# Two joined layers: plain transposes behind row scaling, pairs of attention items, and feed-forward norms applied as r squared behind the second product

## The reference, cut to what matters

```python
# first layer
proj = rmsnorm(x, g_mix_pre) @ w_in            # fq, fk, fv, f_logit, cq, ck, cv
# fox: logits[t,s] = q_t.k_s * scale + c[t] - c[s] (causal), 8 heads of 64
# chk: logits = q.k * scale + rel_bias(table), 8 heads of 64
y = concat([rmsnorm(y_fox, g_fox_out), rmsnorm(y_chk, g_chk_out)])
x = x + rmsnorm(y @ w_out, g_mix_post)
x = x + rmsnorm(attention(rmsnorm(x) @ w_mq, mem_n @ w_mk, mem_n @ w_mv) @ w_mo, g_mem_post)
h = rmsnorm(x, g_ff_pre)
y = jnp.square(jax.nn.relu(h @ w_ff1)) @ w_ff2
x = x + rmsnorm(y, g_ff_post)
# second layer: gated delta rule with a short convolution, sparse attention (dsa) with
# selected keys, two gates, then
x = x + merged @ w_out
h2 = rms_norm(x, norm_mlp_g)
x = x + jnp.square(jax.nn.relu(h2 @ w_mlp_up)) @ w_mlp_down
```

## Time and profile before

| | |
|---|---|
| median of 3 runs | 1035.77 us (1030.82 to 1036.05) |
| the profiled execution, its own time | 1035.79 us |
| its span in the profile | 1034.0 us |
| PE busy | 976.3 us (94%) |
| DVE busy | 589.5 us (57%) |
| ACT busy | 513.9 us (50%) |
| POOL busy | 178.7 us (17%) |
| mean granted clock of PE in the span | 0.98 |

### The profile page before, as it was taken

The page is one execution under the profiler, slowest core; times in us unless marked ns, Lnnn a source line. Parts: engine busy times, 40 slices in busy tenths (PEclk is TensorE's granted clock), DMA queues, the critical chain, the costliest instruction groups (busy, mean ns, idle before and its releaser), DMA issues.

```text
span 1034.0 us, 15468 instructions
## 1 busy us (share of the span) xinstructions
PE 976.3 (94%) x6056; PEld 859.3 (83%) x6056; DVE 589.5 (57%) x921; ACT 513.9 (50%) x910; POOL 178.7 (17%) x171
## 2 busy tenths in 40 slices
PE   5999999999999999999999498999899889999998
PEld 5998876778789998887779497788799879998886
DVE  4353445564466665345578888685554657665342
ACT  4454455564465544335556555754345446544331
POOL 0011000010010000001018888600455200000000
PEclk9998999999999999999999799998999999999999
DMA  9664223244255666563635233263110055655552
GB/s 326 204 196 130 82 82 122 83 157 147 82 162 164 192 196 201 170 199 123 203 113 174 82 123 124 86 200 122 41 42 2 1 163 163 196 172 198 170 201 81
DMA packets 99703, 146.75 MB, mean 142 GB/s; under 512 B 2480, under 2 KB 57904, under 8 KB 99504
## 3 DMA queue, kind: packets, MB, share of 16 engines
q1 hardware_dynamic: 99632, 145.78, 43.6%
HBM read 144.72 MB, written 1.05 MB: 141 GB/s over the span
## 4 chain that ended last, share of the span: by engine, by line
PE 43%; issue 42%; DVE 8%; POOL 2%; ACT 2%; DVEq 1%; DMA 1%; POOLq 1%; SPq 0%; ACTq 0%
PE acc L429 5%; PE acc L430 5%; PE acc L431 5%; PE acc L441 5%; PE acc L442 5%; PE acc L443 5%; DVE s_w_lo L379 3%; PE aux L1509 2%; DVE s_qkvT L1279 1%; ACT s_w_hi L373 1%; PE acc L467 1%; PE acc L468 1%; PE acc L469 1%; PE aux L1439 1%; DMA s_w_raw<-in_w_in 1%
## 5 line engine op out<-in xcount | busy, mean ns | idle before, releaser
L379 DVE TENSOR_TENSOR s_w_lo<-s_w_raw,s_w_hi 128x2048 fp32r<-128x2048 f32 (+1 forms) x195 | 312.5, 1609 | 211.3 <-ACT s_w_hi L373 211.0
L373 ACT ACTIVATE s_w_hi<-s_w_raw 128x2048 fp32r<-128x2048 f32 (+1 forms) x195 | 263.8, 1361 | 144.5 <-PE acc L431 117.5
L441 PE MATMUL acc<-s_h_hi,s_w_hi 128*128 128x256 f32 x800 | 229.4, 287 | 3.1 <-DVE s_h_lo L612 1.8
L442 PE MATMUL acc<-s_h_lo,s_w_hi 128*128 128x256 f32 x800 | 227.4, 284 | 0.0
L443 PE MATMUL acc<-s_h_hi,s_w_lo 128*128 128x256 f32 x800 | 227.3, 284 | 0.0
L441 PEld LDWEIGHTS acc<-s_h_hi,s_w_hi 128*128 128x128 f32 x800 | 154.1, 193 | 4.2 <-DVE s_w_lo L379 2.0
L442 PEld LDWEIGHTS acc<-s_h_lo,s_w_hi 128*128 128x128 f32 x800 | 154.1, 193 | 0.1
L443 PEld LDWEIGHTS acc<-s_h_hi,s_w_lo 128*128 128x128 f32 x800 | 154.1, 193 | 0.0
L430 PE MATMUL acc<-s_w_lo,s_hid_hi 128*128 128x512 f32 x224 | 89.5, 400 | 0.0
L429 PE MATMUL acc<-s_w_hi,s_hid_hi 128*128 128x512 f32 x224 | 88.4, 395 | 0.0
L431 PE MATMUL acc<-s_w_hi,s_hid_lo 128*128 128x512 f32 x224 | 87.8, 392 | 0.0
(11 more groups left out here) (300 smaller groups left out, 1682.7 us busy)
## 6 DMA issues: line engine op xcount, KB each, us to landing
s_w_raw<-in_w_in SPq DMA_DIRECT2D x44, 1024.0 KB, 5.2
s_w_raw<-in_w_ff SPq DMA_DIRECT2D x32, 1024.0 KB, 5.2
s_w_raw<-in_w_mlp_up SPq DMA_DIRECT2D x16, 1024.0 KB, 5.4
s_w_raw<-in_w_mlp_down SPq DMA_DIRECT2D x16, 1024.0 KB, 5.1
s_w_raw<-in_w_out SPq DMA_DIRECT2D x8, 1024.0 KB, 5.1
s_w_raw<-in_w_mk SPq DMA_DIRECT2D x4, 1024.0 KB, 5.0
s_w_raw<-in_w_mv SPq DMA_DIRECT2D x4, 1024.0 KB, 5.1
s_w_raw<-in_w_mq SPq DMA_DIRECT2D x4, 1024.0 KB, 5.2
```

What stands on the lines that cost most here:

```text
L373: act.activation(w_hi[u % SPLIT_SLOTS][:, cs], w_raw[u % RAW_SLOTS][:, cs], ACT.Copy).then_inc(w_hi_done, 4 if q is None else 1)
L379: dve.tensor_tensor(w_lo[u % RAW_SLOTS][:, cs], w_raw[u % RAW_SLOTS][:, cs], w_hi[u % SPLIT_SLOTS][:, cs].bitcast(F32), ALU.subtract).then ...
L441: pe.matmul(o, wh[:, cs], hi[:, k, :], start=k == 0, stop=False)
L442: pe.matmul(o, wh[:, cs], lo[:, k, :], start=False, stop=False)
```

## The change

1. **Norms of x at first and of `mem`.** DVE multiplies the rows by r (128x1024, two instructions) and PE does 16 plain transposes in place of 16 matmuls with the diagonal. At the start ACT and DVE split unit 0 in quarters, with the first rows' split between them, and unit 1 behind.
2. **Fox bias.** The second matmul of each fox item goes. Four matmuls (`fb_pe`, 8 rows, 512 columns) stand between the quarters of cv's second unit, and DVE adds the mask to them once (`fb_dve`), into a bias that the items read.
3. **Attention in pairs.** Items are ordered by tile, then head, and go in pairs: two score products, v products of the pair before the last, transposes of the last pair, then two quarters of weights (three in dsa). Copy and reciprocal are one instruction per pair.
4. **Norm of y by tiles.** Tile 0's squares, scaling and transposes lie in the attention; `out` units 0 and 1 run tile by tile with tile 1's norm between. Memory attention ends likewise before `mo`.
5. **Turns mo to ff1 and out2 to up.** The rows are transposed without r; only the gain is applied (`gain_act`, `gain_dve`). The squares come after the gains, POOL makes r squared (`r2_pool`), and it scales behind `ff2` and `down`. The transposes lie inside the last pair of products.
6. **Delta rule.** Unit 1 of gb moves from behind the back part to between the four `dt_pe` blocks, and a gate (`GATES[9]`) is computed earlier.

```diff
+        def gain_act(act, n, t, g):
+            N.wait(act, nt_tr)
+            for c in range(4):
+                k = 4 * g + c
+                act.activation(h_hi[:, k, t * P:(t + 1) * P], tile_bank(t, g)[:, c * P:(c + 1) * P], ACT.Copy,
+                               scale=gcol[:, GAIN[n], k:k + 1]).then_inc(nt_hi, 1)
...
+        def r2_pool(pool, n, t):
+            c = 4 * NCOL[n] + t
+            pool.wait_ge(ss_done, squares_until(n, 1, t))
+            pool.tensor_scalar(stat[:, c:c + 1], stat[:, c:c + 1], stat[:, c + 2:c + 3], EPS, ALU.add, ALU.add)
+            pool.drain()
+            pool.tensor_tensor(r2_col(n, t), stat[:, c:c + 1], minus1[:], ALU.pow)
+            pool.drain()
+            pool.tensor_scalar(r2_col(n, t, 2), r2_col(n, t), ROOT_D, None, ALU.mult).then_inc(r2_done, 1)
...
+        def nt_dve_scale(dve, n, src, dst):
+            for t in range(NT):
+                N.wait(dve, rstd_done)
+                c = 4 * NCOL[n] + t
+                dve.tensor_scalar(dst[:, t, :], src[:, t, :], rstd[:, c:c + 1], None, ALU.mult).then_inc(diag_done, 1)
...
-                        if GAIN[n] is None:
-                            i = pe.transpose(o, piece, ident())
-                        else:
-                            g = k // 4 if n == "y" else 0
-                            i = pe.matmul(o, piece, diag[:, 2 * g + t, :], start=True, stop=True)
+                        i = pe.transpose(o, piece, ident())
...
+        def y_dve_scale(dve, t, g):
+            N.wait(dve, rstd_done)
+            c = 4 * NCOL["y"] + 2 * t + g
+            piece = y[:, t, g * 512:(g + 1) * 512]
+            dve.tensor_scalar(piece, piece, rstd[:, c:c + 1], None, ALU.mult).then_inc(diag_done, 1)
+        def y_pe(pe, t, g):
+            N.wait(pe, diag_done)
+            for c in range(4):
+                k = 4 * g + c
+                i = pe.transpose(Y_BANK[t][g][:, c * P:(c + 1) * P], y[:, t, k * P:(k + 1) * P], ident())
+            i.then_inc(nt_tr, 1)
...
+            pe.wait_ge(p_done, i + 2)
+            if i:
+                pe.wait_ge(ptc_done, i)
+            nb = it["nk"] // P
+            for j in range(2):
+                for b in range(nb):
+                    m = pe.transpose(PT_BANK[:, (j * nb + b) * P:(j * nb + b + 1) * P], bufs(i)[1][:, (i + j) % 3, b * P:(b + 1) * P], ident())
+            m.then_inc(pt_done, 2)
...
-                                      qk=[(fqT[r:r + 64, m, ts], fkT[r:r + 64, m, 0:nk]), (sel_l[r:r + 40, h, ts], sel_r[r:r + 40, 0:nk])],
-                                      bias=cst[:, C_CAUSAL + 2 * P - nk:C_CAUSAL + 2 * P],
...
+                    items.append(dict(nk=nk, scale=1.0, dv=FD, qk=[(fqT[r:r + 64, m, ts], fkT[r:r + 64, m, 0:nk])],
+                                      bias=foxb[:, h, :] if t else xn[:, 1, h * P:(h + 1) * P],
...
+        def fb_pe(pe, between):
+            for j in range(4):
+                pe.matmul(FB_BANK[j][:], sel_a[0:8, 0:P], sel_l[0:8, 2 * j:2 * j + 2, :], start=True, stop=True).then_inc(fb_mm, 1)
+                between(j)
...
+        def fb_dve(dve):
+            for j in range(4):
+                dve.wait_ge(fb_mm, j + 1)
+                b = FB_BANK[j][:].rearrange("p (h s) -> p h s", h=2)
+                dve.tensor_tensor(xn[:, 1, 2 * j * P:(2 * j + 2) * P].rearrange("p (h s) -> p h s", h=2), b[:, :, 0:P],
+                                  both(cst[:, C_CAUSAL + P:C_CAUSAL + 2 * P]), ALU.add)
+                dve.tensor_tensor(foxb[:, 2 * j:2 * j + 2, :], b, both(cst[:, C_CAUSAL:C_CAUSAL + 2 * P]), ALU.add).then_inc(fb_done, 1)
...
+                dve.scalar_tensor_tensor(xn[:, t, cs], acc[b][:], r2_col("ff", t), gpost[:, cs], ALU.mult, ALU.mult).then_inc(acc_free[b], 1)
...
+        def ff_act(act, tag, post, pre):
+            last = of[tag][-1]
+            for u in of[tag][:-2]:
+                advance_hi(act, u)
+            post_stats(act, post, tag, 0)
+            advance_hi(act, last - 1)
+            post_stats(act, post, tag, 1, [0])
+            for q in (0, 1):
+                advance_hi(act, last, q)
+            for g in range(2):
+                gain_act(act, pre, 0, g)
+            post_stats(act, post, tag, 1, [1])
+            for q in (2, 3):
+                advance_hi(act, last, q)
+            for g in range(2):
+                gain_act(act, pre, 1, g)
+            act.wait_ge(x_done, 2 * NT * 2)
+            for t in range(NT):
+                for g in range(2):
+                    square(act, pre, g, t, x[:, t, g * 512:(g + 1) * 512])
...
-            for i in range(len(items) + 3):
-                if i < len(items):
-                    at_pe_scores(pe, i0 + i, items[i])
-                if 2 <= i <= len(items) + 1:
-                    at_pe_tr(pe, i0 + i - 2, items[i - 2])
-                if i >= 3:
-                    at_pe_pv(pe, i0 + i - 3, items[i - 3])
-                between(i)
+            n = len(items) // 2
+            for p in range(n + 2):
+                if p < n:
+                    for j in (2 * p, 2 * p + 1):
+                        at_pe_scores(pe, i0 + j, items[j])
+                if p >= 2:
+                    at_pe_pv(pe, i0 + 2 * p - 4, items[2 * p - 4:2 * p - 2])
+                if 1 <= p <= n:
+                    at_pe_tr(pe, i0 + 2 * p - 2, items[2 * p - 2])
+                between(p)
...
+        def fox_parts(p):
+            lo, hi = [min(4 * len(MEMU), max(0, 2 * k - 1)) for k in (p, p + 1)]
+            return [(MEMU[q // 4][0], MEMU[q // 4][1], q % 4) for q in range(lo, hi)]
...
-            for u in range(AHEAD):
-                unit_hi(act, u)
+            for q in range(4):
+                unit_hi(act, 0, q)
             act.wait_ge(gain_in, 16)
             nt_act(act, "mix", h_hi)
+            for u in range(1, AHEAD):
+                unit_hi(act, u)
...
+                if p == len(FOX) // 4 + 2:
                     act.wait_ge(y_done, len(FOX) // 2)
-                    for t in range(NT):
-                        square(act, "y", 0, t, y[:, t, 0:512])
+                    for g in range(2):
+                        square(act, "y", g, 0, y[:, 0, g * 512:(g + 1) * 512])
+                if p == 3 * len(FOX) // 8 + 2:
+                    act.wait_ge(y_done, 3 * len(FOX) // 4)
+                    square(act, "y", 0, 1, y[:, 1, 0:512])
+                if p == len(FOX) // 2:
+                    for g in range(2):
+                        y_act(act, 0, g)
...
-                wait_added(act, "out2", 0, t)
-                square(act, "mlp2", 0, t, x[:, t, 0:512])
-            wait_added(act, "out2", 1, 0)
-            square(act, "mlp2", 1, 0, x[:, 0, 512:D])
             for q in (0, 1):
                 advance_hi(act, of["out2"][-1], q)
-            wait_added(act, "out2", 1, 1)
-            square(act, "mlp2", 1, 1, x[:, 1, 512:D])
-            nt_tile_act(act, "mlp2", h_hi, 0, range(KC))
+            for g in range(2):
+                gain_act(act, "mlp2", 0, g)
             for q in (2, 3):
                 advance_hi(act, of["out2"][-1], q)
-            nt_tile_act(act, "mlp2", h_hi, 1, range(KC))
+            for g in range(2):
+                gain_act(act, "mlp2", 1, g)
+            for t in range(NT):
+                for g in range(2):
+                    wait_added(act, "out2", g, t)
+                    square(act, "mlp2", g, t, x[:, t, g * 512:(g + 1) * 512])
...
-            nt_dve_diag(dve, "mix")
-            for u in range(AHEAD):
+            nt_dve_scale(dve, "mix", x, xn)
+            for j in range(2):
+                for q in (2 * j, 2 * j + 1):
+                    unit_lo(dve, 0, q)
+                nt_dve(dve, "mix", h_hi, h_lo, (2 * j, 2 * j + 1))
+            for u in range(1, AHEAD):
...
+            def x_tile(tag, t):
+                for g in range(2):
+                    if tag == "mo":
+                        pe.wait_ge(x_done, 2 * NT + 2 * t + g + 1)
+                    else:
+                        wait_added(pe, tag, g, t)
+                    quad_pe(pe, tile_bank(t, g), x, t, g)
...
+            tile_mm(pe, u0, 0, h_hi, h_lo, fresh)
+            y_pe(pe, 1, 0)
+            tile_mm(pe, u1, 0, h_hi, h_lo, fresh)
             pe.wait_ge(y_done, len(FOX))
-            nt_pe(pe, "y", y, (2, 3))
-            normed[0] += KC
-            mm("out", 0, 1, fresh=True)
+            y_pe(pe, 1, 1)
+            tile_mm(pe, u0, 1, h_hi, h_lo, fresh).then_inc(unit_done, 1)
+            tile_mm(pe, u1, 1, h_hi, h_lo, fresh).then_inc(unit_done, 1)
...
-                if b == 11:
-                    mm("gb", 1)
             for b in range(4):
                 dt_pe(pe, b)
+                mm("gb", 1, parts=[b])
```

More of the change, by code:

```diff
@@ L462, in pair_mm @@
                         k, cs = r["k0"] + kk, slice(kk * 512, (kk + 1) * 512)
+                        if within is not None and (v, kk) == (u + 1, 2):
+                            within(t)
                         if t == 0:
@@ new lines, in at_dve_copy, with at_pe_pv @@
```

(10 more changed lines are left out.)

366 lines of the change are left out of this document (233 added, 133 removed).

## The result

The changed kernel takes 1000.36 us (median of 4 runs, 999.06 to 1001.23) against 1035.72 for the kernel before in the same comparison: ratio 0.967, 95% interval 0.964 to 0.970. The profiled execution's span is 999.4, against 1034.0. The forecast was 1003. In the comparisons of the later runs the kernel before had medians of 1033.55, 1033.24 and 1032.66, so the gain is 32 to 35 us.

A forecast was written before the change was run, and what follows sets the result against it. PE, busy 976.3 of 1034.0 us, was taken to bound the kernel. Terms summing to 33.3 us less gave span 1000.7, time 1002.5, stated as 1003; range 991 to 1016, with 998 to 1008 at 0.57.

The forecast's parts named there:

- The start: First weight product: row scaling and plain transposes let PE start about 3.8 us earlier (2.2 to 4.3).
- mem, bias, the end of y: Transposes at mem 1.9 us less, fewer fox bias matmuls 2.6 less, first attention's end up to out 5.0 less.
- Pairs: First attention: 32 items share 16 switches between attention and weights in place of 32, 2.6 us less.
- The half clock at the attention's start: First attention: the 6.90 us half-clock stretch after the s_cv wait goes, at 6 in 10; 3.4 us less.
- Turns: mo to ff1 1.6 us less, out2 to up 2.5 less, after new w_lo stalls of about 2.1 and 2.2.
- dsa: dsa attention: fewer switches and less idleness, partly given back ahead of L1339; 3.0 us less (1 to 5).
- Delta rule: Earlier gate removes most of the 2.3 us wait ahead of L1522, moved unit gives DVE and ACT time; 2.2 less.
- The half clock that stays or moves: Rival, chance 0.2: the 3.4 us is not won and one or two new half-clock stretches cost 1.7 each; 1006 to 1012.
- Transposes that leave PE at 1.2 GHz: Rival, chance 0.06: half clock after transposes at six places, 1.7 us each; 1013.
- the third rival: Chance 0.1: squares don't stall ff1 and up, delta rule's clock recovers; 4.3 and 3 us better, 994 to 998.
- Pairs that wait: Rival, chance 0.04: in the attentions PE stands once per pair for a chain longer than 2.8 us; 1041 and more.
- the fifth: Rival, chance 0.03: weights or POOL decide and hide the gain, with waits on s_w_raw; within 0.5% of 1036.

The follow-up runs named there:

- e8_start: Changed kernel with the old order of ACT and DVE at the start, transposes and row scaling kept; 1004.57 us, one run.
- e3_heads: Changed kernel with fox and chk heads reordered so both of a pair have their rows in the same half of the partitions; 1004.34 us.
- e1_pad: Kernel before with one unused column allocated, every tile behind it 32 bytes further; 1028.6 us against 1033.55, ratio 0.9965.
- e4_squares: Changed kernel with the four squares at both turns moved behind the next w_hi; 992.93 us against the changed kernel's 1000.36.
- e12: Changed kernel, no edit, profiled once more; 997.93 us, one run.
- e7_taps: Changed kernel with two of the four convolution taps left out on POOL, so the output differs; 996.29 us, one run.
- e10_tanh: Changed kernel with squares behind w_hi, h_hi and h_lo shifted, and the last convolution's tanh and product moved up two blocks; 981.36 us, ratio to before 0.950.
- e9_gb: Changed kernel with gb's unit 1 in one piece again ahead of the dt_pe blocks, earlier gate kept; 997.54 us, one run.
- e11: Kernel before, no edit, profiled once more; 1035.89 us, one run.

## Why the prediction was right, and where a term was not

The total was right, and most terms with it; two terms failed, and their errors have opposite signs.

*The start* was right in size (4.24 for 3.8), and e8_start shows its reason: `h_lo` behind two whole units. The transposes alone bring nothing to the first product.

*mem, bias, the end of y* were right within 0.5 each.

*Pairs* is the term that was mis-sized: forecast 2.6 by the switches alone, measured 9.3. That is what the attention won, 19.5, less the bias (8 by 0.53 and 8 by 0.32, 6.8) and the half clock (3.4), both read from rows. I priced two score products of 64 rows as twice one. They overlap: 5.2 us by the records of e3_heads, 4.7 by its attention as a whole. The other 4.1 are not isolated by a run. The pitch of the attention's weights fell from 0.1187 to 0.1138 for 192 matmuls and from 0.234 to 0.230 for 96, together 1.3, of which e1_pad, with the tiles shifted alone, has about 0.5. That leaves 2.8 for the switches, near the forecast 2.6.

*The half clock at the attention's start* (3.4) came as forecast, but what it had to do with the wait was not as sure as the term has it. In three profiles with the wait of 1.5 us it stands twice; in the eleven profiles with the new order the wait is gone and it never stands.

*Turns.* The moved squares ahead of `w_hi` were forecast to make PE wait for about 2.1 and 2.2 us on `w_lo`. They did, 2.3 each, and e4_squares takes the waits away by moving the squares alone. The forecast's own times (13.9 to 14.6 against 12.6) give 1.3 to 2.0, so the 2.1 written there was the upper end. What I left out is the half clock behind such a wait, 1.5 us each in the profiled execution, none in e12's.

*dsa.* The step that failed is "the convolutions do not become faster, and what PE wins it partly gives back ahead of L1339". The give-back was seen: 3.7 us more of wait (4.6 in e12) and a half clock of 1.4 behind it, less what the stretch of 646 to 650 at half clock in the kernel before gave back. It was larger than priced, and its cause was the written place of the last tanh and of its product behind a `w_hi` and a `w_lo`, and not the convolutions (e7_taps, e10_tanh). The net of the stage was -1.8 for the forecast +3.0, outside its bounds of 1 to 5.

*Delta rule.* 3.1 for 2.2, by another sum: the half clock at `ap_pe` went (3.0), the gate's wait went (2.3), and the interleaved unit cost 2.2 (e9_gb), where I had taken it as free. That the clock there depends on the change is not shown. It stayed full in e9_gb, it was full in e1_pad, which has nothing of the change, and in e11 the kernel before had half of the stretch. The 3.0 are thus in part the luck of which execution of the kernel before was profiled, and what fixes the clock there is open.

*The rivals.* The half clock that stays or moves (0.2) came in part: the one of 6.9 us went, two that cost 1.5 each came, in some executions. Transposes that leave PE at 1.2 GHz (0.06) were not seen: none of the half-clock stretches in the two profiles of the changed kernel stands behind the transposes at the start, at `mem`, at y or at a turn. Only e8_start has one there, 16.3 to 23.1, and it lies behind the transposes and a wait of 4.5 us, which that run does not tell apart. Of the third rival (0.1) the stalls on `w_lo` came after all and the clock at `ap_pe` recovered. Pairs that wait did not come: L767 waits 1.0 once in this attention. PE's waits show none on `s_w_raw`, so the fifth did not come either. The two slips, +6.7 and -4.8, nearly cancel, as do the +3 of the pitch in ff2 and down and the -3 of the new half clocks; the closeness of 1003 to 1000.4 owes much to that and is in so far luck.
